# Score products of two heads issued alternately, softmax taken by pairs

## The reference

```python
h = rmsnorm(x, ln_mix_g)
qa, ka, va, qb, kb, vb, ga, gb = split(h @ w_in)        # rotary on q and k
o_a = moba_attention(qa, ka, va)      # 8 heads of 64; with 256 tokens: plain causal attention
o_b = dilated_attention(qb, kb, vb)   # 4 heads x 3 groups (dilations 1, 4, 16), softmax over all groups' keys
mix = sigmoid(ga + b_gate_a) * (o_a @ w_o_a) + sigmoid(gb + b_gate_b) * (o_b @ w_o_b)
x = x + mix @ w_out
x = x + moe_ffn(rmsnorm(x, ln_ffn_g))  # top 4 of 32 experts, 3 weight matrices of 4 MB each
return rmsnorm(x, ln_final_g)
```

## Time and profile before

| | |
|---|---|
| runs, median (lowest to highest) | 1175.64 us (1173.2 to 1177.0), three runs |
| profiled execution | 1173.92 us, its span 1172.1 us |
| TensorE matmul / weight load busy | 1095.9 us (93%) / 496.3 us (42%) |
| VectorE / ScalarE busy | 300.3 us (26%) / 201.1 us (17%) |
| transfers | 439.43 MB, mean 375 GB/s |
| granted TensorE clock, mean | 0.994 |

### The profile page before, as it was taken

How to read it: one execution, slowest core, us unless ns; L and a number is a source line. 1 busy time by engine, 2 the same in 40 slices (tenths; PEclk the granted TensorE clock), 3 DMA queues, 4 the chain that set the end, 5 groups by cost and what they waited for, 6 DMA issues and landing times.

```text
span 1172.1 us, 11962 instructions
## 1 busy us (share of the span) xinstructions
PE 1095.9 (93%) x5178; PEld 496.3 (42%) x5178; DVE 300.3 (26%) x688; ACT 201.1 (17%) x341; POOL 4.5 (0%) x11
## 2 busy tenths in 40 slices
PE   6999999999999999999999989999999989999986
PEld 5888888533333333333333333333333333333332
DVE  7656656331111111111111111111111111111112
ACT  5345444011111111111111111111111111111101
POOL 0000000000000000000000000000000000000000
PEclk9999999989999999999999999999999999999999
DMA  9744226889999999999999999999999999999993
GB/s 355 244 162 162 93 89 250 346 334 413 428 428 426 428 428 427 427 428 428 428 428 427 426 429 427 428 428 428 428 428 428 426 428 427 429 427 428 427 428 147
DMA packets 44330, 439.43 MB, mean 375 GB/s; under 512 B 3866, under 2 KB 5170, under 8 KB 19700
## 3 DMA queue, kind: packets, MB, share of 16 engines
q1 hardware_dynamic: 44260, 438.64, 89.8%
q10 hardware_dynamic: 16, 0.00, 0.0%
HBM read 437.58 MB, written 1.05 MB: 374 GB/s over the span
## 4 chain that ended last, share of the span: by engine, by line
PE 64%; DMA 32%; issue 2%; DVE 1%; ACT 1%; SPq 0%; POOL 0%; DVEq 0%; POOLq 0%; ACTq 0%
PE ps L851 36%; DMA attn<-in_w_up_dram 10%; DMA wd<-in_w_up_dram 10%; DMA wg<-in_w_up_dram 7%; PE ps L577 4%; DMA wd<-in_w_gate_dram 4%; PE ps L873 3%; PE ps L817 3%; PE ps L763 2%; PE ps L615 2%; PE ps L640 2%; PE ps L607 2%; PE ps L842 1%; PE ps L687 1%; PE ps L688 1%
## 5 line engine op out<-in xcount | busy, mean ns | idle before, releaser
L1241 DVE TENSOR_SCALAR gates<-ps 128x512 f32<-128x512 f32 x32 | 22.1, 691 | 517.8 <-PE ps L851 517.8
L851 PE MATMUL ps<-wd,gates 128*64 128x512 f32 x512 | 115.6, 596 | 10.3 <-DMA wd<-in_w_gate_dram 8.5
L851 PE MATMUL ps<-wg,gates 128*64 128x512 f32 x512 | 115.8, 597 | 3.6 <-DMA wg<-in_w_up_dram 3.4
L851 PE MATMUL ps<-wu,o_t 128*64 128x512 f32 x352 | 78.0, 595 | 7.8 <-issue 4.4
L851 PE MATMUL ps<-attn,gates 128*64 128x512 f32 x352 | 81.5, 605 | 2.9 <-DMA attn<-in_w_up_dram 2.7
L851 PE MATMUL ps<-wu,gates 128*64 128x512 f32 x320 | 72.8, 597 | 5.7 <-DMA wu<-in_w_gate_dram 5.7
L525 ACT ACTIVATE o_t<-ps 128x512 f32<-128x512 f32 x32 | 19.1, 597 | 308.4 <-PE ps L577 308.3
L851 PEld LDWEIGHTS ps<-wd,gates 128*64 128x64 f32 x512 | 36.0, 137 | 82.4 <-issue 63.8
L851 PEld LDWEIGHTS ps<-wg,gates 128*64 128x64 f32 x512 | 35.4, 137 | 71.0 <-issue 62.3
L512 ACT ACTIVATE gates<-gates 128x512 f32<-128x512 f32 x32 | 20.2, 630 | 255.2 <-DVE gates L1241 255.2
L817 PE MATMUL ps<-xs,work 128*64 128x512 f32 x256 | 62.2, 607 | 0.7 <-DVE work L1219 0.7
(11 more groups left out here) (174 smaller groups left out, 1270.9 us busy)
## 6 DMA issues: line engine op xcount, KB each, us to landing
wg<-in_w_up_dram SPq DMA_DIRECT2D x22, 2048.0 KB, 37.3
wu<-in_w_down_dram SPq DMA_DIRECT2D x22, 2048.0 KB, 38.7
wd<-in_w_gate_dram SPq DMA_DIRECT2D x22, 2048.0 KB, 38.0
attn<-in_w_gate_dram SPq DMA_DIRECT2D x11, 2048.0 KB, 37.7
slot_wv<-in_w_gate_dram SPq DMA_DIRECT2D x11, 2048.0 KB, 35.4
slot_xh<-in_w_up_dram SPq DMA_DIRECT2D x11, 2048.0 KB, 39.4
attn<-in_w_up_dram SPq DMA_DIRECT2D x11, 2048.0 KB, 40.2
slot_wv<-in_w_down_dram SPq DMA_DIRECT2D x11, 2048.0 KB, 40.3
```

The source lines that it names most:

```text
L851: mm = pe.matmul(ps[SLOTS * h:SLOTS * h + SLOTS, bank, :], lhs[:, k, :], ring[n % RING][:, r, 512 * h:512 * h + 512], start=(k == 0 and no ...
L1241: dve.tensor_scalar(g_act, ps[:, G, :], LIMIT, None, ALU.min).then_inc(g_ready, 1)
```

## The change

Two score products of a pair are issued alternately, one from the lower half of the partitions, one from the upper half, and a pair's scores are counted once (`scored` goes to 8 instead of 16). Both units of a pair are scored together, inside the even unit's gate tile, behind its first 9 of 24 products, and wait for the copies of both units of the pair before. The values of the pair before now come before the even unit's transposes. VectorE takes the row maxima of both units of a pair before the even one's divide: the odd unit's right before it, the next even unit's behind the odd unit's copy. `row_maxima` also waits for the `row_max` count of the units before. ScalarE's program is the same.

```diff
@@ sync
-            sp.wait_ge(scored, N_UNITS)
+            sp.wait_ge(scored, N_UNITS // 2)
             sp.wait_ge(row_max, n_soft[N_UNITS])
             piece(0, 0)
@@ tensor
-            def scores(u):
+            def score_parts(u):
                 kind, h, b = units[u]
                 base = 2 + 2 * (u % 2)
-                if u >= 2:
-                    pe.wait_ge(p_ready, u - 1)
-                elif u == 1:
-                    pe.wait_ge(proj_read, NB * 8)
                 if kind == "a":
                     r = HD * (h % 2)
                     q, k = qk_t[r:r + HD, QA + h // 2, :], qk_t[r:r + HD, KA + h // 2, :]
+                    return [(ps[:, base, 0:128], q[:, 0:128], k[:, 0:128]),
+                            (ps[:, base, 128:384], q[:, 128:256], k[:, 0:256])]
...
+            def scores(q):
+                if q >= 1:
+                    pe.wait_ge(p_ready, 2 * q)
                 else:
+                    pe.wait_ge(proj_read, NB * 8)
+                for even, odd in zip(score_parts(2 * q), score_parts(2 * q + 1)):
+                    for out_ap, lhs, rhs in (even, odd):
+                        mm = pe.matmul(out_ap, lhs, rhs, start=True, stop=True)
                 mm.then_inc(scored, 1)

-            def gate_tile(t):
+            def gate_tile(t, ks=range(KT)):
...
-            for u in range(N_UNITS):
-                gate_tile(u)
-                if u + 1 < N_UNITS:
-                    scores(u + 1)
-                turn_probs(u)
-                if u >= 2 and u % 2 == 0:
-                    weigh_values(u // 2 - 1)
+            gate_tile(0)
+            for q in range(N_UNITS // 2):
+                if q >= 1:
+                    weigh_values(q - 1)
+                turn_probs(2 * q)
+                gate_tile(2 * q + 1)
+                turn_probs(2 * q + 1)
+                if q + 1 < N_UNITS // 2:
+                    gate_tile(2 * q + 2, range(0, 3))
+                    scores(q + 1)
+                    gate_tile(2 * q + 2, range(3, KT))
             weigh_values(N_UNITS // 2 - 1)
@@ vector
-                dve.wait_ge(scored, u + 1)
+                dve.wait_ge(scored, u // 2 + 1)
                 if u >= 2:
                     dve.wait_ge(exp_done, n_soft[u - 1])
+                if u >= 1:
+                    dve.wait_ge(row_max, n_soft[u])
...
             for u in range(N_UNITS):
+                if u % 2 == 0:
+                    row_maxima(u + 1)
                 divide(u)
-                if u + 1 < N_UNITS:
-                    row_maxima(u + 1)
                 for c, q in parts_after(u):
                     split_lo(c, q)
                 probs_out(u)
+                if u % 2 == 1 and u + 1 < N_UNITS:
+                    row_maxima(u + 1)
```

More of the change, by code:

```diff
@@ L662, in scores @@
                     q, k = qk_t[r:r + HD, QA + h // 2, :], qk_t[r:r + HD, KA + h // 2, :]
-                    pe.matmul(ps[:, base, 0:128], q[:, 0:128], k[:, 0:128], start=True, stop=True)
-                    mm = pe.matmul(ps[:, base, 128:384], q[:, 128:256], k[:, 0:256], start=True, stop=True)
-                else:
[L666 to L673, removed]
+                    return [(ps[:, base, 0:128], q[:, 0:128], k[:, 0:128]),
+                            (ps[:, base, 128:384], q[:, 128:256], k[:, 0:256])]
@@ new lines, in score_parts @@
+                keys = P * (b + 1)
+                parts = []
+                for g in range(NG):
+                    hh = HEADS_G * g + h
+                    r = HD * (hh % 2)
+                    q, k = qk_t[r:r + HD, QB + hh // 2, :], qk_t[r:r + HD, KB + hh // 2, :]
+                    at = g * keys
+                    parts.append((ps[:, base + at // 512, at % 512:at % 512 + keys], q[:, P * b:P * b + P], k[:, 0:keys]))
+                return parts
+            def scores(q):
+                if q >= 1:
+                    pe.wait_ge(p_ready, 2 * q)
+                else:
+                    pe.wait_ge(proj_read, NB * 8)
+                for even, odd in zip(score_parts(2 * q), score_parts(2 * q + 1)):
+                    for out_ap, lhs, rhs in (even, odd):
+                        mm = pe.matmul(out_ap, lhs, rhs, start=True, stop=True)
@@ L674, in scores @@
                 mm.then_inc(scored, 1)
-            def gate_tile(t):
+            def gate_tile(t, ks=range(KT)):
                 c = GATE_CHUNK0 + t // 4
[L678 to L684, removed]
+                if ks[0] == 0:
+                    if t % 4 == 0:
+                        pe.wait_ge(hi_ready, PARTS * (c + 1))
+                        pe.wait_ge(lo_ready, PARTS * (c + 1))
+                    if t >= 2:
+                        pe.wait_ge(gate_read, t - 1)
+                    elif t == 0:
+                        pe.wait_ge(proj_read, NB * 7)
@@ L685, in gate_tile @@
                 cut = slice(P * (t % 4), P * (t % 4) + P)
-                for k in range(KT):
+                for k in ks:
                     pe.matmul(ps[:, t % 2, 0:SEQ], w_hi[:, c % 2, k, cut], h_hi[:, :, k, :], start=(k == 0), stop=False)
@@ L690, in gate_tile @@
                                    start=False, stop=(k == KT - 1))
-                mm.then_inc(gate_done, 1)
+                if ks[-1] == KT - 1:
+                    mm.then_inc(gate_done, 1)
             def turn_probs(u):
```

## The result

The change makes the kernel slower by 0.6%, where 0.4% was forecast.

A forecast was written before the change was run, and what follows sets the result against it. TensorE's own work was taken to bound attention, and the expert-weight stream the last 900 us. Terms -6.4 - 2.6 + 0.55 + 13.4 = +5.0 us gave 1180.6 us against the median 1175.64; range 1176.5 to 1187.

The forecast's parts named there:

- The savings: TensorE in attention: 6.4 us from overlapping score products and 2.6 from fewer changes of shape, 9.0 less work.
- The overlap of the row halves: Paired score products in attention: full overlap of the two heads, saving 0.64 us in six pairs, 1.29 in two.
- The 0.97: One pair's scores in attention: one overlap (0.64 us) plus one change of shape (0.33) saved.
- The waits: TensorE in attention: new waits for VectorE's results at four kinds of places, 13.4 us added.
- (a): Before scores of pairs 1, 3, 5, 7: wait for the odd copy behind split_lo, 1.85 us each, 7.4 in all.
- (d): First round: transposes wait 1.5 us instead of 0.5, behind the bias split, two row maxima and a divide; 1.1 new.
- (c): Before even units' transposes: both row maxima precede the divide; 0.28 us three times, 0.50 twice, 1.8 in all.
- (b): Before transposes of units 3, 7, 11, 15: even unit's two splits delay them 0.95 us twice, 0.89 twice; 3.7, 3.1 new.
- the sum of 5.0: Whole kernel: savings and added waits together make it 5.0 us slower.
- Nothing absorbs it: 185 to 255 us: attention's delay passes on whole; the rival, weight stream hides it, gave 1175.6 us, chance 0.07.
- Loads one behind the other: Rival, paired scores in attention: operand loads cannot run together, 2.1 us lost, +7.1, 1182.7 us; chance 0.14.
- The clock: Rival, new pauses in attention: clock falls to half, costing up to 4.6 us, about 1185; chance 0.04.

The follow-up runs named there:

- e6: Changed kernel plus 14 gate-sized products before gate tiles 2, 6, 10, 14 and small products in the last round's two pauses: 1180.48 us, ratio 1.0059.
- e3: Changed kernel plus 14 gate-sized products ahead of the scores of pairs 1, 3, 5 and 7: 1179.76 us, ratio 1.0043 to the kernel before.
- e1: Changed kernel with the odd unit's probability copy ahead of its split_lo on VectorE: 1171.12 us, ratio 0.9981 to the kernel before.
- e2: Changed kernel with all score products of one head, then the other's, instead of alternately: 1186.24 us, ratio 1.0088 to the kernel before.
- e4: Changed kernel with VectorE's and ScalarE's queues also ordered by pairs: 1170.29 us, ratio 0.9960 to the kernel before.
- e5: Changed kernel with three gate products between the two heads' scores in every pair: 1196.10 us, ratio 1.0181 to the kernel before.
- e7: e4 with the bias split moved behind the first pair's divides and exps: 1169.06 us, ratio 0.9960 to the kernel before.

## Why the prediction was right, and where it was wrong

Marks of TensorE, read off the issues that SyncE has queued behind them, show where each kernel stands against before (us; minus is earlier):

| SyncE's issue, time in before | after | e6 | e3 |
|---|---|---|---|
| L356, 138.22 | +5.31 | +3.51 | +3.54 |
| L332 behind `pv_done`, 183.95 | +7.64 | +5.15 | +6.13 |
| L332 behind `oproj_done`, 201.41 | +8.44 | +5.14 | +6.69 |
| L332, 234.44 | +8.44 | +5.13 | +6.69 |
| L332, 249.12 | +7.09 | +5.11 | +5.20 |
| L332 `wu`, 268.36 | +8.78 | +5.11 | +5.21 |

Three of these issues in after, as the trace has them:

```profile
191.59 0.34 SPq L332 DMA_DIRECT2D slot_wv<-in_w_gate_dram  x1
...
209.85 0.82 SPq L332 DMA_DIRECT2D wg<-in_w_up_dram  x2
...
256.21 0.33 SPq L332 DMA_DIRECT2D attn<-in_w_up_dram  x1
```

And the stretches at half clock, from the record of the granted clock (start, length in us; without the one at the very end that each profile has):

| | stretches at 0.50 |
|---|---|
| before | 236.7 (10.2) |
| after | 114.8 (3.4), 189.9 (3.4), 244.5 (6.8), 271.8 (3.4) |
| e1 | 232.5 (6.8), 867.4 (3.4) |
| e2 | 114.9 (3.4), 244.6 (6.8), 282.1 (6.8), 306.0 (3.4) |
| e3 | 187.8 (3.4), 242.5 (6.8), 280.0 (6.8), 303.9 (3.4), 802.2 (3.4), 1058.2 (3.4) |
| e4 | 230.1 (6.8) |
| e5 | 114.5 (6.8), 162.3 (6.8), 189.6 (10.2), 257.9 (6.8), 295.4 (6.8), 319.3 (3.4) |
| e6 | 241.7 (10.2), 1112.1 (3.4) |
| e7 | 231.0 (6.8), 258.3 (3.4) |

*The savings: right.* The overlap of the row halves, for which the trace before had no row, is whole: in after the two heads' passes of 768 columns start at 155.994 and 156.001, 156.314 and 156.321, and so on in pairs 6 to 7 ns apart, from the second on 0.216 us from pair to pair. The Trainium skill, TensorE: Matmul & The Clock Gate, Part 3, has products in different row groups start some 4 ns apart; the trace comes near that, with 6 to 7 ns, and that they need not be issued in turn is what e2 adds. The 0.97 of e5's undisturbed round is 1.05. In size the saving was somewhat overrated: TensorE is 8.2 us less busy in e1 (72.42 against 80.59) and 8.5 in e4, both at full clock, where 9.0 was said.

*The waits: right.* (a) 7.4 worked out, 7.4 measured, four times; e1 shows that the copy's place behind split_lo makes it. The nine waits before transposes, 6.3 us, split as foreseen: (d) 1.41 where 1.5 was said; (c) 0.50, 0.37, 0.53 and 0.51 us, 1.9 for 1.8; (b) 1.08, 0.64, 0.62 and 0.63, 3.0 for 3.7, of which 0.17 each was to lie under the tail of a product, where the profile shows no idle time. That (c) comes out so close is partly luck: five waits were said, and the first is missing in after, where TensorE is slow at that moment (half clock to 118.2). In e3, at full clock there, all five stand, 0.38, 0.49, 0.38, 0.53 and 0.53, 2.3 us, and the first of (b) is 0.64 instead of 1.08. The wait before the last value products stays at 1.05. With it TensorE idles 14.7 us in after (89.56 less 74.87) and 1.9 before: 12.8 more, for 13.4. So the sum of 5.0 holds by two small misses that nearly cancel, a saving of 8.2 for 9.0 and waits of 12.8 for 13.4: 0.57 - 8.2 + 12.8 = 5.2, where e6 has 5.15.

*Nothing absorbs it: right.* In e6 the shift is 5.15 at `pv_done` and 5.11 at 249.12 and at 268.36, and e4's gain comes through to the end (span 1166.1 against 1172.1 us). The weight stream sets the pace behind 265 us but waits for TensorE before.

*Loads one behind the other: wrong, though its number is the result.* It gave 1182.7, and 1182.89 was measured. The trace excludes it: two loads of 186 ns start at 156.101 and 156.108, side by side, and a pair of twelve passes takes 1.57 us. Who has only the end time would take the false rival for the cause.

*The clock: the step that failed.* The sentence was "pauses of 1.9 us hardly exceed today's last one", and the term was set to nothing. The comparison does not hold even by its own rows: today's last pause is 1.05 us, and 1.85 is 1.8 times that, and there are four of them. The profile of after has the clock at half right behind such a pause, from 114.81 (scores started at 113.97 after 1.84 us of idle time) and from 189.90 (value products at 189.28, behind 0.63 and 1.05 us of idle time). The 15 gate products behind the first pause reach from 114.83 to 117.98, 3.15 us where the same 15 at full clock take 1.77 (126.00 to 127.77): 1.4 us for one fall.

In the table of marks after stands 1.80 behind e6 at 138.22, of which 0.32 is a later first score (101.92 against 101.60), then 2.49 at `pv_done` and 3.30 at `oproj_done`. By 249 it has got back 1.35, its long fall there being 6.8 us instead of the 10.2 of before and e6, and the fall at 271.8 costs it 1.7 again.

For the medians it is a mean: the granted clock over a whole run was 0.9908 on average in after's 20 runs and 0.9932 in 41 runs of before; 0.0024 less, twice that of 1182 us, is 5.7 us more at half clock. After's own runs go from about 1178 at a clock of 0.995 to 1188.09 at 0.986; the difference of 0.009 is 21 us more at half clock for 10 us of time, some 0.45 a microsecond. So 5.7 us cost 2.6, and 5.0 + 2.6 = 7.6 of the 7.9. The prediction had priced the case at up to 4.6 and given it 0.04. That the time lies in the range all the same is owed to the room that the range kept for other rivals, up to 1187.

The part of it in attention is seen in e6 and not only summed: with work added to a waiting TensorE the group behind attention comes 2.5 us earlier. The split of the medians by the mean clock is an estimate, but the mean clock is no matter of one profile. By kernel it is, over all runs:

| four pauses of 1.84 us | runs | mean clock | no such pause | runs | mean clock |
|---|---|---|---|---|---|
| after | 20 | 0.9908 | before | 41 | 0.9932 |
| e2 | 6 | 0.9902 | e1 | 12 | 0.9938 |
| e5 (three of 1.84, one of 1.36) | 5 | 0.9844 | e3 | 9 | 0.9927 |
| | | | e4 | 10 | 0.9933 |
| | | | e6 | 6 | 0.9927 |
| | | | e7 | 12 | 0.9933 |

Every kernel with the pauses lies under every one without them. What the chip decides by is not shown. The timeline of TensorE in after has the same pause three times more, with full clock behind it:

```profile
136.01 0.93 PE L680 MATMUL ps<-attn 64*128 64x128 f32 x8 [1.84 <-DVE work L1099]
...
178.12 1.57 PE L680 MATMUL ps<-attn 64*128 64x256 f32 x12 [1.84 <-DVE work L1099]
```

(the third is at 155.99, above). One of four such pauses is followed by a fall, in e2 as well, and three of four in e5. Without the pause the fall is gone, as e1, e3 and e6 show, but the pause alone does not bring it. The same goes for the last round: its two pauses (0.62 and 1.05 us) have a fall behind them in after and e3, and none in e1 and e2, where they are as long. So e6, which filled them and has no fall there, does not show in one profile that the filling was what removed it. And the falls between 257 and 320 us, present in the profiles of after, e2, e3, e5 and e7 and absent in those of before, e1, e4 and e6, lie in the first experts, where no kernel here differs from another. One profile of each is too little to say whether they belong to the kernels; they stay open.

## What to carry to other kernels

When work is regrouped on the engine that bounds a stage, walk the queues of the other engines with the new deadlines, not with their busy shares: here more than 8 us of TensorE's work were saved, and VectorE and ScalarE, busy 68% and 54% of the stage before (56.34 and 44.23 of 82.49 us), took back 13, 7.4 of them because a copy stood behind a split that it had nothing to do with. The cure was an order, not less work (e4: 4.7 us under before, 12.6 under after, with the instructions of after). And a pause on TensorE costs more than its length when the clock falls behind it: give that a price, from the rows at half clock, even when the pauses look like old ones. Here it was 1.4 to 1.7 us for 3.4 us at half clock, and 2.6 us of the median by the estimate above.

## What the runs showed that had not been expected

- Products for different halves of the rows overlap without being issued alternately: eight passes, head after head, take 0.93 us as when alternating, twelve take 2.10 instead of 1.57, since up to three waiting passes of one half are run past.
- The granted clock falls for 3.4, 6.8 or 10.2 us, in attention each time behind a pause of 1.4 to 1.8 us or of 0.6 and 1.05 close together; each 3.4 us cost 1.4 to 1.7 us of a busy TensorE. Three pauses of the same length in the same kernel had no fall behind them.
- Three gate products between the heads (e5) turned 7 us of half clock in and right behind attention into 24, with no longer pause anywhere. That has no explanation here.
